# Expert down products moved behind the next block's gate and up products, with h kept in DRAM meanwhile

## The chip, the cores and the metric

The kernel runs on one core of a Trainium2 chip. The metric is the time of one launch in device microseconds: median 2381.64 us of three runs (2381.1 to 2393.33). All times below without a unit are microseconds.

## The reference

One layer of a decoder trunk for 1024 prompt rows and 8 decode rows, D = 1024: projection and two kinds of attention, a residual add, then a mixture of experts, a gated per-layer embedding and a last norm. The change touches what follows the attention:

```python
x = x + hier_moe(rmsnorm(x, g_moe), ...)        # 4 groups x 8 experts, top 2 inside the top group
gate = jax.nn.sigmoid(rmsnorm(x, g_ple) @ w_pg)
x = x + gate * (p @ w_pp);  y = rmsnorm(x, g_final)

def expert_block(args):                          # one block: 128 rows of one expert
    xi, ei = args
    return (jax.nn.silu(xi @ w_gate[ei]) * (xi @ w_up[ei])) @ w_down[ei]
```

`w_gate[e]` and `w_up[e]` are 1024 x 512 floats (2 MiB each), `w_down[e]` is 512 x 1024 (2 MiB). Every block brings its three matrices from HBM, whether or not its neighbour has the same expert.

## The kernel before

The program is a row of stages with a barrier of all engines between them. Four of them matter here: `residual` makes h (9 tiles of 128 rows, the last of 8) and the router's logits; `route` sorts the rows by expert and scatters them to `xs` in DRAM; `experts` works through the blocks; `finish` gathers each row's two results from `ys`, adds them to h and does the rest. h stays in SBUF from `residual` to `finish`.

In this profiled execution `experts` has 32 blocks, two to a turn of a hardware loop (the number comes from a register, `passes`). Each engine has its own in-order instruction stream, and semaphores join them. For block n:

- SP (the queue of loads, in order): x(n), two halves of w_gate, two of w_up, then w_down. The raw w_gate and w_up have one buffer each, so each half waits until VectorE has finished reading the last block's (`gl_full`, `ul_full`). w_down has two buffers and waits for the products of block n - 2.
- ScalarE makes the high parts (`high`: `wgh`, `wuh`, `xh`, type fp32r), VectorE the low parts (`low`: what is left after the high part is taken away). The gate and up products are three fp32r matmuls for each of 8 slices of the contraction (`products`, L86 to L88).
- TensorE (`step`, L1857): `gate_up(n-1)`, `turn(n)` (8 transposes of x), `down(n-1)`: 4 transposes of the hidden rows (L1847), then, when VectorE has copied them to `hT` (L1947), 8 plain fp32 matmuls into two banks (L1854; the profile records each as two).
- VectorE (`step`, L1949): `gated`, the first half of w_gate's low part, `hidden`, `hidden_T`, `turn`, the second half, `low_x`, then w_up's low parts.
- ScalarE copies the result to `y` (L1891), and GpSimd sends it to `ys` (L1981).

A matmul tile is named out<-moving,stationary: `x_Y<-x_wd,x_hT` streams the weights past the transposed hidden rows.

Of the kernel before, what the change touches and what calls it, by code (L numbers as in the profile page):

```python
# [19 lines left out]
P = 128  # L20
# [29 lines left out]
MAXBLK = (ASG + NE * (P - 1)) // P  # L50
NEG = -1.0e30
# [1381 lines left out]
def residual(nc, g, x_of):  # L1433

    ctx = ExitStack()
    with ctx:
# [3 lines left out]
        w = sb("r_w", [P, KD, D])  # L1440
        wr = sb("r_wr", [P, KD, NR])
# [14 lines left out]
        h, u2, logit, mT, ident = g["h"], g["u2"], g["logit"], g["mT"], g["ident"]  # L1456
# [4 lines left out]
        def _(sp):  # L1461
# [9 lines left out]
            for t in range(TT):  # L1471
                need(sp, h_full, t - 1)
                sp.dma_start(xt[0:rows(t), t % 2, :], x_of(t)).then_inc(x_in[t % 2], 16)

# [75 lines left out]
def route(nc, g):  # L1550
# [5 lines left out]
    with ctx:  # L1556
# [95 lines left out]
        def _(dve):  # L1652
# [85 lines left out]
            then(dve.tensor_scalar(metaf[:, 2:3], metaf[:, 2:3], -1.0, None, ALU.add))  # L1738
# [3 lines left out]
def experts(nc, g):  # L1742
# [6 lines left out]
    with ctx:  # L1749
# [17 lines left out]
        x_in, d_in = ([sem(f"{n}{b}") for b in range(2)] for n in ("x_in", "d_in"))  # L1767
        wg_in, wu_in = ([sem(f"{n}{b}") for b in range(2)] for n in ("wg_in", "wu_in"))
        gh_full, gl_full, uh_full, ul_full, xh_full, xl_full = map(sem, (
            "gh_full", "gl_full", "uh_full", "ul_full", "xh_full", "xl_full"))  # L1770
        HALVES = [slice(0, KD // 2), slice(KD // 2, KD)]
        y_out = g["pool_dma"][3:5]
        gm_in, tpx_full, xT_full, g_full, u_full, sg_full, gs_full, hm_full, tph_full, hT_full, y_full, y_read = map(
            sem, ("gm_in", "tpx_full", "xT_full", "g_full", "u_full", "sg_full", "gs_full", "hm_full", "tph_full",
                  "hT_full", "y_full", "y_read"))
        xs, ys, meta_row, ident = g["xs"], g["ys"], g["meta_row"], g["ident"]
        Wg = g["w_gate"].rearrange("a e (k p) f -> (a e) p k f", p=P)
        Wu = g["w_up"].rearrange("a e (k p) f -> (a e) p k f", p=P)
        Wd = g["w_down"].rearrange("a e (k p) f -> (a e) p k f", p=P)
        block = ctx.enter_context(nc.Block())  # L1780

        def pairs(eng):

            return eng.value_load(meta_row[0:1, 2:3], min_val=(-(-ASG // P) + 1) // 2 - 1,
                                  max_val=(MAXBLK + 1) // 2 - 1) + 1

        def passes(eng, step, end):


            n = pairs(eng)  # L1790
            for j in range(2):
                step(0, j)
            with eng.Fori(1, n) as it:
                for j in range(2):
                    step(it, j)
            if end:
                end(n)

        @block.sync
        def _(sp):  # L1800
            with nc.allow_non_contiguous_dma(reason="1024 gains, once"):
                sp.dma_start(gm[:, :], g["g_moe"].rearrange("a (k p) -> p (a k)", p=P)).then_inc(gm_in, 16)

            def step(it, b):
# [11 lines left out]
                need(sp, y_full, it * 4 + (2 * b - 2))  # L1816
# [5 lines left out]
        def _(pe):  # L1822
            def turn(it, b):

                pe.wait_ge(x_in[b], it * 16 + 16)
                for c in range(2):
                    need(pe, xT_full, it * 4 + (2 * b + c - 1))
                    for k in range(4):
                        last = pe.transpose(tpx[c][:, k, :], x[:, b, (c * 4 + k) * P:(c * 4 + k + 1) * P], ident[:, :])
                    last.then_inc(tpx_full, 1)  # L1830

            def gate_up(n):

                pe.wait_ge(xl_full, n + 1)
                need(pe, hm_full, n)
                for bank, wh, wl, cut, s in ((G, wgh, wgl, gl_full, g_full), (U_, wuh, wul, ul_full, u_full)):
                    pe.wait_ge(cut, n * 2 + 2)
                    for k in range(KD):
                        last = products(pe, bank[:, :], xh[:, k, :], xl[:, k, :], wh[:, k, :], wl[:, k, :],
                                        k == 0, k == KD - 1)  # L1840
                    last.then_inc(s, 1)

            def down(p_, b, n):
                pe.wait_ge(hm_full, n + 1)
                need(pe, hT_full, n)
                for k in range(KF):
                    last = pe.transpose(tph[:, k, :], hm[:, k * P:(k + 1) * P], ident[:, :])  # L1847
                last.then_inc(tph_full, 1)
                pe.wait_ge(d_in[b], p_ * 16 + 16)
                pe.wait_ge(hT_full, n + 1)  # L1850
                for c in range(2):
                    need(pe, y_read, n * 2 - 1 + c)
                    for k in range(KF):
                        last = pe.matmul(Y[c][:, :], hT[:, k, :], wd[:, b, k, c * 512:(c + 1) * 512],  # L1854
                                         start=(k == 0), stop=(k == KF - 1))
                    last.then_inc(y_full, 1)

            def step(it, j):
                behind = j or not isinstance(it, int)
                p_, b, n = (it, 0, it * 2) if j else (it - 1, 1, it * 2 - 1)  # L1860
                if behind:
                    gate_up(n)
                turn(it, j)
                if behind:
                    down(p_, b, n)

            def end(np_):
                gate_up(np_ * 2 - 1)
                down(np_ - 1, 1, np_ * 2 - 1)
# [4 lines left out]
        def _(act):  # L1874
# [12 lines left out]
            def output(p_, b, n):  # L1887
                act.wait_ge(y_out[b], p_ * 16 + 16)
                for c in range(2):
                    act.wait_ge(y_full, n * 2 + c + 1)  # L1890
                    act.activation(y[:, b, c * 512:(c + 1) * 512], Y[c][:, :], ACT.Copy).then_inc(y_read, 1)  # L1891

            def step(it, j):
                behind = j or not isinstance(it, int)
                p_, b, n = (it, 0, it * 2) if j else (it - 1, 1, it * 2 - 1)
                new = it * 2 + j
                if behind:
                    sigmoid(n)
                high(new, wg, wgh, wg_in, g_full, gh_full)
                act.wait_ge(xT_full, new * 2 + 2)  # L1900
                act.activation(xh[:, :, :], xT[:, :, :], ACT.Copy).then_inc(xh_full, 1)
                high(new, wu, wuh, wu_in, u_full, uh_full)
                if behind:
                    output(p_, b, n)

            def end(np_):
                sigmoid(np_ * 2 - 1)
                output(np_ - 1, 1, np_ * 2 - 1)
# [4 lines left out]
        def _(dve):  # L1913
            dve.wait_ge(gm_in, 16)

            def turn(n):
                need(dve, u_full, n)
                for c in range(2):
                    dve.wait_ge(tpx_full, n * 2 + c + 1)
# [8 lines left out]
            def low(n, half, w, wh, wl, high_full, full):  # L1928

                dve.wait_ge(high_full, n * 2 + half + 1)  # L1930
# [3 lines left out]
            def gated(n):  # L1934
                dve.wait_ge(sg_full, n + 1)
                dve.tensor_tensor(gs[:, :], sg[:, :], G[:, :], ALU.mult).then_inc(gs_full, 1)
# [7 lines left out]
            def hidden_T(n):  # L1944
                dve.wait_ge(tph_full, n + 1)
                need(dve, y_full, n * 2)
                dve.tensor_copy(hT[:, :, :], tph[:, :, :]).then_inc(hT_full, 1)  # L1947

            def step(it, j):  # L1949
                behind = j or not isinstance(it, int)  # L1950
                n, new = it * 2 - 1 + j, it * 2 + j
                if behind:
                    gated(n)
                low(new, 0, wg, wgh, wgl, gh_full, gl_full)
                if behind:
# [8 lines left out]
            def end(np_):  # L1964
                gated(np_ * 2 - 1)
                hidden(np_ * 2 - 1)
                hidden_T(np_ * 2 - 1)
# [4 lines left out]
        def _(pool):  # L1972
            def step(it, b):
                n = it * 2 + b
                row = pool.value_load(meta_row[0:1, bass.ds(n * 4 + 1, 1)], min_val=0, max_val=ASG)
                pool.wait_ge(y_read, n * 2 + 2)
                if b:
                    pool.wait_ge(y_out[0], it * 16 + 32)
                else:
                    pool.wait_ge(y_out[1], it * 16 + 16)  # L1980
                pool.dma_start(ys[bass.ds(row, P), :], y[:, b, :]).then_inc(y_out[b], 16)  # L1981

            def end(np_):
                for b in range(2):
                    pool.wait_ge(y_out[b], np_ * 16 + 16)
                pool.wait_ge(gm_in, 16)

            passes(pool, step, end)


def finish(nc, g, p_of, y_of):
# [3 lines left out]
    with ctx:  # L1995
# [4 lines left out]
        C = D // 2  # L2000
        wpgh, wpgl = (sb(n, [P, KD, D], F32R) for n in ("wpgh", "wpgl"))
# [27 lines left out]
        h, wt, dest, ys, ident = (g[n] for n in ("h", "wt", "dest", "ys", "ident"))  # L2029
# [12 lines left out]
        def _(sp):  # L2042
            with nc.allow_non_contiguous_dma(reason="1024 gains, once"):
                sp.dma_start(gp[:, :], g["g_ple"].rearrange("a (k p) -> p (a k)", p=P)).then_inc(gp_in, 16)
            for t in range(2):
                sp.dma_start(pt[0:rows(t), t % 2, :], p_of(t)).then_inc(p_in[t % 2], 16)
            for n, (raw, w, _, _) in enumerate(pieces):
                need(sp, wl_full, n - 2)
                sp.dma_start(raw, w).then_inc(piece_in[n], 16)
            sp.dma_start(gf[:, :], g["g_final"].unsqueeze(0).broadcast_to([P, D])).then_inc(gf_in, 16)  # L2050
# [114 lines left out]
        def _(dve):  # L2165
            dve.wait_ge(gp_in, 16)

            def mixed(t):

                r = rows(t)  # L2170
                dve.wait_ge(y_in[t % 2], 32 * (t // 2 + 1))
# [81 lines left out]
def build(nc, g):  # L2253
    ctx = ExitStack()
    with ctx:
# [11 lines left out]
        g["ys"] = nc.dram_tensor("ys", (SLOTS, D), F32, kind="Internal").ap()  # L2267
        g["meta"] = nc.dram_tensor("meta", (P, 4), I32, kind="Internal").ap()
# [22 lines left out]
        with nc.sbuf_tensor("u2", [P, TT, D], F32) as u2:  # L2291
# [18 lines left out]
            g["h"] = ctx.enter_context(nc.sbuf_tensor("h", [P, TT, D], F32, side="right"))  # L2310
# [40 lines left out]
```

## Time and profile before

| What | us |
|---|---|
| Median of the runs | 2381.64 |
| The profiled execution's own time | 2380.5 |
| Its span, first to last instruction | 2378.9 |
| First gate product of the expert stage starts | 1521.57 |
| Last copy of a down product starts | 2194.16 |

Busy shares of the span: TensorE 85%, its weight loads 66%, VectorE 46%, ScalarE 36%, GpSimd 12%. These are means over all stages. For the change the expert stage is read by itself: TensorE is busy about 95 of each 100 us there, and the 16 DMA engines have something to do for about 95% of it. A DMA engine counts as busy while it has a transfer open, so this share says more of how long transfers are open than of how much room is left; the GB/s beside it say what moved. Start times are microseconds from the span's start.

### The profile page before, as it was taken

Reading aid. Unit: us, or ns where it says so; the run is one execution under the profiler, and the core shown is the slowest. Engines: PE = TensorE matmul, PEld = TensorE weight load, DVE = VectorE, ACT = ScalarE, POOL = GpSimd, SP = SyncE. Lnnn points to the kernel's source line nnn. Section 1 sums busy time; section 2 is a strip of 40 time slices with the busy share of each in tenths; the row PEclk is TensorE's granted clock in tenths of the full one; section 3 lists DMA queues with packets and bytes.
Section 4 is the critical chain, followed back from the end, with each engine's and each line's share of the span. In section 5 each row is a group of like instructions: output and inputs, shape, how many; then the busy total and the mean of one; then the engine's idle time right before and its main releaser. Section 6 shows DMA issues by size and latency. Waiting matters only on the chain. (4 is left out here: it accounts for less than half of the span.)

```text
span 2378.9 us, 27707 instructions
## 1 busy us (share of the span) xinstructions
PE 2012.9 (85%) x10172; PEld 1572.0 (66%) x10172; DVE 1098.7 (46%) x1363; ACT 850.9 (36%) x1171; POOL 277.5 (12%) x356
## 2 busy tenths in 40 slices
PE   6999999698989879993288994499999999998598
PEld 5999999687878857772177452366666666665485
DVE  5212121255546545552342214466666666664564
ACT  4111111255546415450031100344444444452354
POOL 0110111143334310001012002100000000000210
PEclk8999999899999959896588996699999999999699
DMA  3343443434111042206334102999999999994530
GB/s 116 113 136 106 124 123 108 144 107 145 37 63 37 28 89 41 41 1 162 102 106 163 53 19 73 341 374 360 348 347 350 352 353 357 351 349 156 194 99 37
DMA packets 222238, 392.70 MB, mean 165 GB/s; under 512 B 29468, under 2 KB 100620, under 8 KB 222165
## 3 DMA queue, kind: packets, MB, share of 16 engines
q1 hardware_dynamic: 202916, 325.28, 40.3%
q0 software_dynamic: 14928, 50.60, 6.7%
q10 hardware_dynamic: 4320, 15.85, 1.7%
q8 instruction: 46, 0.75, 0.1%
q14 instruction: 28, 0.22, 0.0%
HBM read 321.02 MB, written 78.35 MB: 168 GB/s over the span
## 5 line engine op out<-in xcount | busy, mean ns | idle before, releaser
L1854 PE MATMUL x_Y<-x_wd,x_hT 128*128 128x512 f32 x512 | 229.8, 602 | 34.4 <-DVE x_hT L1947 34.4
L86 PE MATMUL p_acc<-uh,p_wl 128*128 128x344 f32 x720 | 234.9, 326 | 13.2 <-DVE ul L292 9.1
L88 PE MATMUL p_acc<-uh,p_wh 128*128 128x344 f32 x720 | 230.6, 320 | 0.0
L87 PE MATMUL p_acc<-ul,p_wh 128*128 128x344 f32 x720 | 230.4, 320 | 0.0
L1854 PEld LDWEIGHTS x_Y<-x_wd,x_hT 128*128 128x128 f32 x512 | 95.2, 191 | 150.1 <-issue 150.1
L304 DVE COPY p_zk<-p_tp 128x512 f32<-128x512 f32 (+1 forms) x90 | 44.2, 547 | 304.5 <-PE p_tp L225 304.5
L1932 DVE TENSOR_TENSOR x_wgl<-x_wg,x_wgh 128x2048 fp32r<-128x2048 f32 x64 | 146.3, 2286 | 69.9 <-ACT x_wgh L1885 69.9
L268 ACT ACTIVATE p_zc<-p_acc 128x344 f32<-128x344 f32 x90 | 41.2, 458 | 321.8 <-PE p_acc L88 321.8
L561 PE MATMUL g_acc<-uh,g_wl 128*128 128x344 f32 x384 | 131.2, 342 | 21.6 <-ACT u L594 19.5
L86 PEld LDWEIGHTS p_acc<-uh,p_wl 128*128 128x128 f32 x720 | 135.8, 189 | 18.1 <-issue 14.8
L1932 DVE TENSOR_TENSOR x_wul<-x_wu,x_wuh 128x2048 fp32r<-128x2048 f32 x64 | 143.5, 2282 | 0.0
L1485 PE MATMUL r_acc<-r_w,mT 128*128 128x512 f32 (+1 forms) x288 | 128.5, 606 | 10.0 <-DMA r_w<-in_w_out 10.0
L1885 ACT ACTIVATE x_wgh<-x_wg 128x2048 fp32r<-128x2048 f32 x64 | 118.9, 1906 | 49.1 <-DMA x_wg<-in_w_gate 49.1
L88 PEld LDWEIGHTS p_acc<-uh,p_wh 128*128 128x128 f32 x720 | 135.9, 189 | 0.0
L87 PEld LDWEIGHTS p_acc<-ul,p_wh 128*128 128x128 f32 x720 | 135.9, 189 | 0.0
L561 PE MATMUL g_acc<-ul,g_wh 128*128 128x344 f32 x384 | 129.7, 338 | 0.0
L561 PE MATMUL g_acc<-uh,g_wh 128*128 128x344 f32 x384 | 129.5, 337 | 0.0
L86 PE MATMUL x_G<-x_wgh,x_xl 128*128 128x512 f32 x256 | 114.8, 448 | 9.9 <-DVE x_xl L1926 9.9
L1885 ACT ACTIVATE x_wuh<-x_wu 128x2048 fp32r<-128x2048 f32 x64 | 118.4, 1896 | 0.1
L655 POOL TENSOR_TENSOR s_z<-s_z,s_w 128x1024 f32<-128x1024 f32 (+7 forms) x64 | 91.8, 1434 | 208.9 <-DVE s_w L682 208.9
L682 DVE TENSOR_TENSOR_SCAN s_w<-s_w,s_r 128x1024 f32<-128x1024 f32 (+7 forms) x64 | 86.8, 1356 | 54.9 <-ACT s_w L631 54.4
L820 PE MATMUL d_S<-d_k,d_q 64*128 64x256 f32 (+3 forms) x272 | 94.8, 499 | 17.4 <-DMA d_v<-ztok 16.9
(320 smaller groups left out, 4089.2 us busy)
## 6 DMA issues: line engine op xcount, KB each, us to landing
x_wg<-in_w_gate SPq DMA_DIRECT2D x64, 1024.0 KB, 7.3
x_wu<-in_w_up SPq DMA_DIRECT2D x64, 1024.0 KB, 7.3
x_wd<-in_w_down SPq DMA_DIRECT2D x32, 2048.0 KB, 12.1
x_x<-xs SPq DMA_DIRECT2D x32, 512.0 KB, 9.8
ys<-x_y POOLq DMA_DIRECT2D x32, 512.0 KB, 5.5
zT<-p_zc ACTq DMA_DIRECT2D x30, 516.0 KB, 3.4
p_w<-in_w_in SPq DMA_DIRECT2D x30, 512.0 KB, 5.5
ztok<-p_zk POOLq DMA_DIRECT2D x30, 512.0 KB, 4.6
```

The lines of the kernel that those rows point to most:

```text
L86: pe.matmul(out, w_low, m_high, start=first, stop=False)
L87: pe.matmul(out, w_high, m_low, start=False, stop=False)
L88: return pe.matmul(out, w_high, m_high, start=False, stop=last)
L304: dve.tensor_copy(zk[0:r, b, t0:t0 + m, :], tp[j % 2][0:r, 0:m, :]).then_inc(zk_full, 1)
L561: last = pe.matmul(acc[grp % 2][:, 0:NS], lhs[:, c % 2, kk, :], rhs[:, kk, t], start=(x == 0), stop=(x == M - 1), skip_group_check=True)
L655: pool.tensor_tensor(z[:, u % ZB, 0:n], z[:, u % ZB, 0:n], w[:, u % WB, 0:n], ALU.subtract).then_inc(al_full, 1)
L682: dve.tensor_tensor_scan(w[:, u % WB, 0:n][:, ::-1], w[:, u % WB, 0:n][:, ::-1], r[:, u % 2, 0:n][:, ::-1], 0.0, ALU.add, ALU.add).then_in ...
L820: last = pe.matmul(S[x // 2][:, c:c + n], q[:, b, x, i * P:(i + 1) * P], k[:, b, x, key:key + n], start=True, stop=True, skip_group_check= ...
L1485: last = pe.matmul(acc[t % 2][0:r, c * 512:(c + 1) * 512], mT[:, k, t * P:t * P + r], w[:, k, c * 512:(c + 1) * 512], start=(k == 0), stop ...
L1854: last = pe.matmul(Y[c][:, :], hT[:, k, :], wd[:, b, k, c * 512:(c + 1) * 512], start=(k == 0), stop=(k == KF - 1))
L1885: act.activation(wh[:, HALVES[half], :], w[:, HALVES[half], :], ACT.Copy).then_inc(full, 1)
L1932: dve.tensor_tensor(wl[:, s, :], w[:, s, :], wh[:, s, :], ALU.subtract).then_inc(full, 1)
```

## The change

1. TensorE works on three blocks at once. Its step n is `gate(n-1)`, `turn_hidden(n-2)`, `up(n-1)`, `turn(n)`, `down(n-2)`. Two steps (one block each) more are peeled from the loop (`PEEL = 2`), and the value that the loop length comes from is shifted (`MINPAIR`).
2. SP's w_down wait is on `d_used`, which `down` raises once per block; the number is still "all blocks up to n - 2".
3. VectorE does both halves of w_gate's low part before `hidden` and `turn`; `hidden_T` goes ahead of them.
4. ScalarE copies out block n - 3 first in its step n, and issues the DMA to `ys` itself, with the load of the row number from SBUF that this needs. GpSimd only waits at the end.
5. The contraction index is split "(p k)" instead of "(k p)" for all three weights, for the gains and for x and the hidden rows: a partition's rows of a half of w_gate lie side by side in DRAM (8 KiB instead of four runs of 2 KiB; w_down 16 KiB instead of four of 4 KiB), and the transposes read their stationary operand with a step of 8 (x) or 4 (hidden rows) floats instead of 1.
6. `residual` has its own h and stores each tile to `h_kept` in DRAM; `finish` loads it again, tiles 0 and 1 ahead of its weights, tiles 2 to 8 behind them and ahead of `gf` (the last norm's gains), and adds a wait for it in `mixed`.

```diff
 sync, experts
-                need(sp, y_full, it * 4 + (2 * b - 2))
+                need(sp, d_used, it * 2 + (b - 1))
                 sp.dma_start(wd[:, b, :, :], w(Wd)).then_inc(d_in[b], 16)
...
-        Wg = g["w_gate"].rearrange("a e (k p) f -> (a e) p k f", p=P)
+        Wg = g["w_gate"].rearrange("a e (p k) f -> (a e) p k f", p=P)
...
 tensor, experts
             def step(it, j):
-                behind = j or not isinstance(it, int)
-                p_, b, n = (it, 0, it * 2) if j else (it - 1, 1, it * 2 - 1)
-                if behind:
-                    gate_up(n)
-                turn(it, j)
-                if behind:
-                    down(p_, b, n)
+                one, two = lag(it, j, 1), lag(it, j, 2)
+                if one:
+                    gate(one[0])
+                if two:
+                    turn_hidden(two[0])
+                if one:
+                    up(one[0])
+                turn(it * 2 + j, j, it)
+                if two:
+                    down(*two)
...
 scalar, experts
+            def output(n, b, it):
+                act.wait_ge(d_used, n + 1)
...
+                row = act.value_load(meta_row[0:1, bass.ds(n * 4 + 1, 1)], min_val=0, max_val=ASG)
+                act.dma_start(ys[bass.ds(row, P), :], y[:, b, :]).then_inc(y_out[b], 16)
...
 vector, experts
-                low(new, 0, wg, wgh, wgl, gh_full, gl_full)
-                if behind:
-                    hidden(n)
-                    hidden_T(n)
-                turn(new)
-                low(new, 1, wg, wgh, wgl, gh_full, gl_full)
+                if two:
+                    hidden_T(two[0])
+                for half in range(2):
+                    low(new, half, wg, wgh, wgl, gh_full, gl_full)
+                if one:
+                    hidden(one[0])
+                turn(new)
                 low_x(new)
...
 sync, finish
             for n, (raw, w, _, _) in enumerate(pieces):
                 need(sp, wl_full, n - 2)
                 sp.dma_start(raw, w).then_inc(piece_in[n], 16)
+            for t in range(2, TT):
+                load_h(t)
             sp.dma_start(gf[:, :], g["g_final"].unsqueeze(0).broadcast_to([P, D])).then_inc(gf_in, 16)
```

On TensorE, in the loop of the kernel before, the end of the up products of a block and what follows (`x_tpx` is the transpose of the new block's x, `x_tph` of the hidden rows):

```order
2182 L88 MATMUL x_U<-x_wuh,x_xh 128x512
2183 L1825 ISA
2184 L59 ISA
2185 L1829 MATMUL x_tpx<-ident,x_x 128x128 x8
2186 L1847 MATMUL x_tph<-ident,x_hm 128x128 x4
2187 L1849 ISA
2188 L59 REGISTER_ALU
2189 L1854 MATMUL x_Y<-x_wd,x_hT 128x512 x8
```

The same engine in the changed kernel, the last peeled step:

```order
2203 L89 MATMUL x_G<-x_wgh,x_xh 128x512
2204 L1868 MATMUL x_tph<-ident,x_hm 128x128 x4
2205 L87 MATMUL x_U<-x_wuh,x_xl 128x512
...
2228 L89 MATMUL x_U<-x_wuh,x_xh 128x512
2229 L1843 MATMUL x_tpx<-ident,x_x 128x128 x8
2230 L1877 MATMUL x_Y<-x_wd,x_hT 128x512 x8
```

The transposes of the hidden rows and the down products that need them now have a block's up products between them, and the down products are those of one block earlier.

On VectorE, one block of the kernel before, from the gated product (`x_gs`) on:

```order
788 L1936 TENSOR_TENSOR x_gs<-x_sg,x_G 128x512
790 L1932 TENSOR_TENSOR x_wgl<-x_wg,x_wgh 128x2048
792 L1942 TENSOR_TENSOR x_hm<-x_gs,x_U 128x512
794 L1947 COPY x_hT<-x_tph 128x512
795 L1920 TENSOR_TENSOR x_xT<-x_tpx,x_gm 128x512
797 L1920 TENSOR_TENSOR x_xT<-x_tpx,x_gm 128x512
798 L1932 TENSOR_TENSOR x_wgl<-x_wg,x_wgh 128x2048
800 L1926 TENSOR_TENSOR x_xl<-x_xT,x_xh 128x1024
```

And in the changed kernel:

```order
800 L1974 TENSOR_TENSOR x_gs<-x_sg,x_G 128x512
802 L1985 COPY x_hT<-x_tph 128x512
804 L1969 TENSOR_TENSOR x_wgl<-x_wg,x_wgh 128x2048
806 L1969 TENSOR_TENSOR x_wgl<-x_wg,x_wgh 128x2048
807 L1980 TENSOR_TENSOR x_hm<-x_gs,x_U 128x512
808 L1957 TENSOR_TENSOR x_xT<-x_tpx,x_gm 128x512 x2
810 L1963 TENSOR_TENSOR x_xl<-x_xT,x_xh 128x1024
```

The second low part of w_gate has moved ahead of the hidden rows (`x_hm`) and of x's transposes (`x_xT`), which stand in front of `x_xl`, the last thing that a block's gate products wait for.

## Rows read from the trace of the kernel before

**Rows 1.** Windows: length, busy us (count) of PE, PEld, DVE, ACT, POOL, PEclk, DMA share, GB/s.
```profile
1522.00:1524.00 2.00, 2.00 (x6) 1.52 (x6) 2.00 (x2) 1.98 (x2) 0.00 (x0) 0.50 1.04 412
1700.00:1800.00 100.00, 94.74 (x364) 63.27 (x363) 65.25 (x49) 46.76 (x38) 2.66 (x5) 1.00 0.95 351
2186.00:2188.00 2.00, 2.00 (x4) 0.91 (x3) 0.00 (x0) 0.00 (x0) 0.00 (x0) 0.50 0.00 0
2250.00:2300.00 50.00, 50.00 (x241) 41.52 (x240) 34.17 (x45) 30.54 (x46) 9.54 (x7) 1.00 0.38 124
```

**Rows 2.** Waits of all engines, 1550 to 2160: who, releaser, total, times, longest.
```profile
PE x_Y L1854 <- DVE x_hT L1947: 31.5, 29, 1.4
```

**Rows 3.** Waits of SP, same stretch.
```profile
SPq L1815 <- DVE x_wgl L1932: 297.9, 58, 6.3
```

**Rows 4.** Timeline of one block: start, duration, engine, line, operation, tile, idle before.
```profile
1753.35 0.79 PE L86 MATMUL x_G<-x_wgh,x_xl 128*128 128x512 f32 x1
...
1764.94 1.03 PE L1829 MATMUL x_tpx<-ident,x_x 128*128 128x128 f32 x8
1765.97 0.66 PE L1847 MATMUL x_tph<-ident,x_hm 128*128 128x128 f32 x4
1767.48 1.28 DVE L1920 TENSOR_TENSOR x_xT<-x_tpx,x_gm 128x512 f32<-128x512 f32 x2
1767.80 7.13 PE L1854 MATMUL x_Y<-x_wd,x_hT 128*128 128x512 f32 x16 [1.18 <-DVE x_hT L1947]
1768.68 2.28 DVE L1932 TENSOR_TENSOR x_wgl<-x_wg,x_wgh 128x2048 fp32r<-128x2048 f32 x1
1768.79 1.06 ACT L1901 ACTIVATE x_xh<-x_xT 128x1024 fp32r<-128x1024 f32 x1 [4.97 <-DVE x_xT L1920]
1770.88 1.22 DVE L1926 TENSOR_TENSOR x_xl<-x_xT,x_xh 128x1024 fp32r<-128x1024 f32 x1
...
1774.37 0.79 PE L86 MATMUL x_G<-x_wgh,x_xl 128*128 128x512 f32 x1
```

**Rows 5.** SP's own timeline of the same stretch.
```profile
1755.97 0.46 SPq L1817 DMA_DIRECT2D x_wd<-in_w_down  x1
...
1764.51 6.98 SPq L1815 DMA_DIRECT2D x_wg<-in_w_gate  x2
```

**Rows 6.** Tile x_wg: its loads, from issue to landing.
```profile
DMA to landing us min/median/max: 4.9/7.3/14.1
```

**Rows 7.** Timeline, first block: ScalarE released by the two halves of w_gate.
```profile
1512.75 1.91 ACT L1885 ACTIVATE x_wgh<-x_wg 128x2048 fp32r<-128x2048 f32 x1 [46.79 <-DMA x_wg<-in_w_gate]
...
1515.42 1.91 ACT L1885 ACTIVATE x_wgh<-x_wg 128x2048 fp32r<-128x2048 f32 x1 [0.76 <-DMA x_wg<-in_w_gate]
```

**Rows 8.** Timeline: the first gate products, and the last block.
```profile
1521.57 0.79 PE L86 MATMUL x_G<-x_wgh,x_xl 128*128 128x512 f32 x1 [9.88 <-DVE x_xl L1926]
...
1526.85 0.46 PE L86 MATMUL x_G<-x_wgh,x_xl 128*128 128x512 f32 x1
...
2183.59 0.66 PE L1847 MATMUL x_tph<-ident,x_hm 128*128 128x128 f32 x4 [0.87 <-DVE x_hm L1942]
2185.30 8.83 PE L1854 MATMUL x_Y<-x_wd,x_hT 128*128 128x512 f32 x16 [1.06 <-DVE x_hT L1947]
...
2194.16 0.60 ACT L1891 ACTIVATE x_y<-x_Y 128x512 f32<-128x512 f32 x1 [2.84 <-PE x_Y L1854]
```

**Rows 9.** Page, DMA issues, one of the last stage: KB each, us to landing.
```profile
f_gf<-in_g_final SPq DMA_DIRECT2D x1, 512.0 KB, 9.0
```

**Rows 10.** Timelines of SP, VectorE and TensorE in the last stage.
```profile
2230.84 0.47 SPq L2050 DMA_DIRECT2D f_gf<-in_g_final  x1
...
2242.70 1.22 DVE L2194 TENSOR_TENSOR f_uT<-f_tp,f_gp 128x1024 f32<-128x1024 f32 x1
...
2250.70 0.75 DVE L2186 TENSOR_SCALAR f_un<-h,f_st 128x1024 f32<-128x1024 f32 x1
...
2251.53 1.07 PE L2084 MATMUL f_tp<-ident,f_un 128*128 128x128 f32 x8
```

More of the change, by code:

```diff
@@ L50 @@
 MAXBLK = (ASG + NE * (P - 1)) // P
+MINPAIR = (-(-ASG // P) + 1) // 2
 NEG = -1.0e30
@@ L1780, in experts @@
         block = ctx.enter_context(nc.Block())
-        def pairs(eng):
-            return eng.value_load(meta_row[0:1, 2:3], min_val=(-(-ASG // P) + 1) // 2 - 1,
-                                  max_val=(MAXBLK + 1) // 2 - 1) + 1
+        PEEL = 2
         def passes(eng, step, end):
[L1790 to L1793, printed above, removed]
+            n = eng.value_load(meta_row[0:1, 2:3], min_val=0, max_val=(MAXBLK + 1) // 2 - MINPAIR) + MINPAIR
+            for it in range(PEEL):
+                for j in range(2):
+                    step(it, j)
+            with eng.Fori(PEEL, n) as it:
@@ L1797, in passes, with lag @@
                 end(n)
+        def lag(it, j, back):
+            new = it * 2 + j
+            if isinstance(it, int) and new < back:
+                return None
+            return new - back, (j - back) % 2, it + (j - back) // 2
         @block.sync
@@ L1830, in turn, with gate_or_up, gate @@
                     last.then_inc(tpx_full, 1)
-            def gate_up(n):
+            def gate_or_up(n, bank, wh, wl, cut, full):
+                for k in range(KD):
+                    if k % 4 == 0:
+                        pe.wait_ge(cut, n * 2 + (k // 4 + 1))
+                    last = products(pe, bank[:, :], xh[:, k, :], xl[:, k, :], wh[:, k, :], wl[:, k, :],
+                                    k == 0, k == KD - 1)
+                last.then_inc(full, 1)
+            def gate(n):
                 pe.wait_ge(xl_full, n + 1)
+                need(pe, gs_full, n)
+                gate_or_up(n, G, wgh, wgl, gl_full, g_full)
@@ L1835, in gate_up, with up @@
+            def up(n):
                 need(pe, hm_full, n)
[L1836 to L1843, printed above, removed]
+                gate_or_up(n, U_, wuh, wul, ul_full, u_full)
@@ L1871, in _ @@
+                if two:
[5 more added lines that the diff above has]
+                    down(*two)
+            def end(np_):
+                last = np_ * 2 - 1
+                gate(last)
+                turn_hidden(last - 1)
+                up(last)
+                down(last - 1, 0, np_ - 1)
+                turn_hidden(last)
+                down(last, 1, np_ - 1)
             passes(pe, step, end)
@@ L1964, in end @@
             def end(np_):
-                gated(np_ * 2 - 1)
-                hidden(np_ * 2 - 1)
-                hidden_T(np_ * 2 - 1)
+                last = np_ * 2 - 1
+                gated(last)
+                hidden_T(last - 1)
+                hidden(last)
+                hidden_T(last)
             passes(dve, step, end)
@@ L1972, in _ @@
         def _(pool):
[L1973 to L1988, printed above, removed]
+            np_ = pool.value_load(meta_row[0:1, 2:3], min_val=0, max_val=(MAXBLK + 1) // 2 - MINPAIR) + MINPAIR
+            for b in range(2):
+                pool.wait_ge(y_out[b], np_ * 16)
+            pool.wait_ge(gm_in, 16)
 def finish(nc, g, p_of, y_of):
@@ L2000, in finish @@
         C = D // 2
+        h = sb("h", [P, TT, D])
+        hs_in = [sem(f"h_in{t}") for t in range(TT)]
         wpgh, wpgl = (sb(n, [P, KD, D], F32R) for n in ("wpgh", "wpgl"))
```

102 lines of the change are left out of this document (59 added, 43 removed).

## The prediction

> **What bounds the kernel now.** I read the windows first, to find the stage that the change works in: in the middle of the expert stage TensorE is busy 94.7 of 100 us at full clock, while 351 GB/s move [rows 1]. The waits come next: TensorE's one wait there is for the copy of the transposed hidden rows, 29 times, 31.5 us together [rows 2]; it never waits for a weight. The timeline of one block gives its step [rows 4]: gate and up products 1753.35 to 1764.94 (11.59), transposes of x 1.03, transposes of the hidden rows 0.66, the wait up to 1767.80 (1.17), down products to the next gate product at 1774.37 (6.57). Together 21.02, of which 19.85 are work. So the stage is bound by TensorE, and the reader should see in [rows 3] why loads never matter: SP waits only for VectorE to free the raw weights, never for the down products. The w_down of a block goes out at 1755.97 and the next block's w_gate at 1764.51 [rows 5].
>
> The expert stage lasts from 1521.57 to the end of the last copy at 2194.76, 673.2 us [rows 8].
>
> **What the new order of TensorE gives.** The hidden rows' transposes are followed by up products of 5.8 us instead of by products that need their copy. The 1.17 wait is hidden. If that were all, a step would last 19.85, and 31 blocks would give back about 36 us. Total work is the same: the down products are the same 8 plain fp32 matmuls.
>
> **What it takes: SP.** Call D the end of the down products of block n - 2. In the kernel before they end in TensorE's step n - 1; now they end in step n, one step later, while SP's wait for them still stands at the same place, in front of w_down(n). Behind this wait in SP's order are x(n+1) and both halves of w_gate(n+1), whose buffers VectorE freed long before. They used to leave then; now they leave at D, and behind 2.10 MB of w_down and 0.52 MB of x. ScalarE's result DMA (0.52 MB) is issued after its two copies, at about D + 3, and shares the engines in just this stretch. From D to the first gate product of block n + 1:
>
> - issue and latency 2.2: the quickest w_gate half took 4.9 [rows 6], of which 1.05 MB at 393 GB/s (the two halves of the first block landed 2.67 apart, [rows 7]) are 2.7;
> - 2.10 + 0.52 + 2.10 + 0.52 = 5.24 MB. The rate for rows of 8 and 16 KiB isn't in the trace. With rows of 2 and 4 KiB it was 393 by the landings and 412 in the best window [rows 1, 7]; at 393 it would be 13.3; larger rows may gain as much again over 412 as that is above 393 (431), which gives 12.2. I take 405, between the two measured ones: 12.9;
> - high part of the second half 1.91 [rows 7], its low part 2.28, then on VectorE the hidden rows 0.65 (the size of one of x's two, 1.28 for both), x's transposes 1.28, on ScalarE xh 1.06, on VectorE xl 1.22 [rows 4]; hand-overs of some 0.1 each, 0.4. Together 8.8.
>
> Sum 23.9. TensorE would be ready for that gate product at D + 19.85, so it waits 4.1. It comes in every second interval: D(n-2) holds back gate n+1, whose step ends with D(n) 19.85 later. Two blocks last 19.85 + 23.9 = 43.8 at least, against 42.0 now.
>
> **The clock.** In the last block TensorE stood 0.87 and 1.06 around 0.66 of work, and then ran the next stretch at a granted clock of 0.50, the 1.2 GHz level [rows 1, 8]; its 16 down records took 8.83 instead of 7.13, 1.7 lost. At the stage's start 12 gate products at this level took 5.28 (1521.57 to 1526.85) instead of 2.80, 2.5 lost. The gaps of 1.2 in the middle of the stage leave the clock at 1.00 [rows 1]. A wait of 4.1 is longer than the last block's two together, so I expect the fall each time, and 2.0 lost, between the two rows. Bounds: 0 and 2.5.
>
> **The sum of the stage.** Behind w_gate(0), in at 1515.4 [rows 7], come w_up(0), w_down(0), x(1) and w_gate(1), 6.8 MB, so w_gate(1) is in at 1515.4 + 6.8 / 0.405 = 1532.2, and with 8.8 the second gate product starts at 1541.0. The third starts at 1560.9. From there to the 32nd: 15 intervals of 23.9 + 2.0 and 14 of 19.85 give 666.4, so 2227.3. Then 11.59 + 0.66 + 6.57 + 0.66 + 1.17 + 7.13, and 1.2 for two copies after the end: 29.0, ending at 2256.3. That is 61.5 later than 2194.76.
>
> **Transposes with a step of 8 and 4 floats.** Each is 0.13 (1.03 / 8) now [rows 4]; no row has a strided stationary operand. Bounds: nothing, and twice the time, 1.69 more in a step. It would count only in the interval that TensorE bounds: 15 times, 25 us. I take nothing, as in the nearest rows. The Trainium skill (SBUF — State Buffer, Specifications (TRN2), Cachelines) says that a 16-byte line has to be hit at least twice for full bandwidth and that each cross to a new line pays a penalty; both steps cross at every float. By this rule the strided transposes would be slower, which is the last rival below; no row here bears it out or refutes it.
>
> **Result rows from ScalarE.** Two copies, a register load and an issue fit ahead of the sigmoid: ScalarE is busy 46.8 of 100 us [rows 1]. I take nothing beyond the 0.52 MB counted above; if they came late they would hold up the sigmoid, which has until D + 15 before it matters. GpSimd's queue held nothing else.
>
> **h through DRAM.** The stores (4.2 MB) lie in `residual`, beside TensorE's work: nothing; the last lands some 3 us after h is made, and the stage still works on logits then. In the last stage tiles 0 and 1 arrive beside the gathers: nothing, at most 2.6 (1.05 MB). But tiles 2 to 8 (3.18 MB) now go out in front of `gf`, which was issued at 2230.84 and took 9.0, so it landed at 2239.8 [rows 9, 10]. VectorE waits for it in front of the loop. It began at 2242.70; with 3.18 MB at 0.405, 7.9 later, gf lands at 2247.7, and VectorE starts 5.0 late. Its un of tile 2 (ended 2251.45) met TensorE's transposes at 2251.53 with 0.08 to spare, and TensorE is busy all of the next 50 us [rows 1, 10]. So 5.0 are added, and 0 to 2.5 for the clock: 6.5.
>
> **Sum.** 2380.5 (the profiled execution's time; its span is 2378.9, and the median is 1.1 above it) + 61.5 + 6.5 = 2448.5; I say 2448.
>
> **Rivals.**
>
> - The clock stays at its upper level over the waits of 4 us. For it: the wait is a single one, and between waits TensorE is busy without a break. Against it: the last block. Then 15 x 2.0 and 1.5 less: 2417.
> - SP's wait binds nothing and TensorE bounds the stage. Faster. Place: the gate product after D. It holds if the second half of w_gate(n+1) lands by D + 11.0 (19.85 - 8.8), where I count 15.1. For it: two blocks' worth of time look like enough slack, large rows may move faster than any row here, and 351 GB/s are less than 412. Against: even at 431 GB/s and without the result rows it is D + 2.2 + 11.0. Then 1560.9 + 29 x 19.85 + 29.0 = 2165.6, 29.2 earlier, with 6.5 lost at the end: 2358.
> - Between: the loads land at about D + 13, without the result rows in their way; a wait of 2 us that leaves the clock alone. 15 x 21.8: 1560.9 + 327 + 277.9 + 29.0 = 2194.8, as before, with the 6.5 of the last stage: 2387.
> - Slower still: transposes at twice the time on top of the forecast, 2448 + 25 = 2473.
>
> The Trainium skill (DMA: Bandwidth & Descriptors, Where 436 GB/s comes from) puts the ceiling of the DMA ports at 435 GB/s. With that instead of 405 the long interval would be 0.9 shorter and the forecast 13 less; the windows here reach 412.
>
> **How the numbers follow.** Forecast 0.50, full clock 0.20, the faster case 0.12, the one between 0.08, slow transposes 0.10. A measurement of this kernel can tell about 0.5%, 12 us. The faster case alone is faster (0.12); the one between falls on both sides of 2394, mostly in no change (0.06); the rest is slower (0.82). The range reaches from 2386, which leaves out the faster case and a little of the one between, to 2474. The likeliest case's own range is 2425 to 2465.
>
> **What would show it.** SP waiting for TensorE's x_Y in front of x_wd, 29 times some 14 to 16 us; x_wg's two issues close together right behind x_x. TensorE waiting for VectorE's x_xl in front of x_G, about 15 times 4 us, long and short block intervals alternating (near 26 and 20); granted clock under 1.00 in windows of the stage. No wait for x_hT within the loop. In the last stage VectorE held at f_uT until 2247 + the shift of the stage. x_tpx in 1.03 or not. The prediction is wrong if SP doesn't wait for TensorE, or if w_gate lands within 11 us of D.

## The result and the profile after

| | median, us | runs |
|---|---|---|
| before | 2385.80 | 2381.10 to 2393.33, 4 |
| after | 2472.81 | 2463.96 to 2478.21, 4 |

The ratio is 1.0358, 95% interval 1.0313 to 1.0403: slower. The forecast of 2448 had the direction and lies 25 under the median. The median is inside the stated range of 2386 to 2474, by 1.2, and above the likeliest case's own range of 2425 to 2465, by 8. The profiled execution of after took 2478.21, its span is 2476.6. Two more executions of each kernel were profiled later, to see what of the difference repeats. Cut at the same four places (the first load of x, the first gate product, the end of the last copy of a down product, the first load of the last stage), the spans read:

| Piece | before, 3 executions | after, 3 executions | mean difference | forecast |
|---|---|---|---|---|
| up to the first load of x | 1506.1, 1525.2, 1521.2 | 1529.7, 1530.8, 1513.2 | +7.1 | 0 |
| first load to first gate product | 15.5, 15.5, 16.0 | 16.6, 17.1, 16.9 | +1.2 | 0 |
| first gate product to the end of the last copy | 673.2, 672.9, 673.1 | 740.9, 736.3, 735.7 | +64.6 | +61.5 |
| end of the last copy to the last stage's first load | 6.8, 6.8, 6.8 | 3.9, 3.9, 3.9 | -2.9 | 0 |
| last stage | 177.3, 177.3, 177.7 | 185.5, 186.8, 185.1 | +8.4 | +6.5 |

The pieces from the first load of x on repeat, within 0.5 in before and 5.2 in after. They add up to +71.3, against 68.0 in the forecast. The piece ahead of them does not repeat, and takes up the rest.

The middle of the expert stage, windows of after (columns as in [rows 1]):

```profile
1700.00:1800.00 100.00, 86.96 (x315) 60.23 (x316) 59.31 (x45) 45.69 (x37) 0.00 (x0) 0.92 0.82 325
...
1748.00:1750.00 2.00, 0.23 (x1) 0.23 (x2) 1.23 (x1) 2.00 (x3) 0.00 (x0) 1.00 1.02 434
1750.00:1752.00 2.00, 2.00 (x6) 1.57 (x6) 1.88 (x1) 2.00 (x3) 0.00 (x0) 0.57 0.89 379
1752.00:1754.00 2.00, 2.00 (x7) 1.53 (x6) 2.00 (x2) 0.85 (x2) 0.00 (x0) 0.58 1.06 440
```

TensorE is busy 87 of 100 us where it was 95, at 0.92 of full clock where it had 1.00, and the DMA engines moved 325 GB/s where they moved 351. Nothing is nearer its limit than before; everything waits more. The waits of after, from 1560 to 2230 (who waits <- for whom, total, times, longest):

```profile
ACT x_wgh L1916 <- DMA x_wg<-in_w_gate: 105.2, 29, 7.2
PE x_G L87 <- DVE x_xl L1963: 72.3, 15, 5.1
```

And those of SP's queue in the same stretch, which answer to [rows 3]:

```profile
SPq L1830 <- PE x_Y L1877: 440.2, 28, 17.1
SPq L1828 <- DVE x_wul L1969: 85.9, 30, 6.5
```

The wait of [rows 2] for `x_hT` is gone. In its place TensorE waits every second block for `x_xl`, and behind that ScalarE waits for the w_gate load itself. The load is late because SP stood in front of w_down for up to 17.1. One block of SP, then of ScalarE and VectorE, then of TensorE, each in order of time (start, duration, engine, line, operation, tile, idle before); they answer to [rows 4, 5]:

```profile
1725.67 0.33 SPq L1830 DMA_DIRECT2D x_wd<-in_w_down  x1
1727.51 0.33 SPq L1824 DMA_DIRECT2D x_x<-xs  x1
1728.10 0.91 SPq L1828 DMA_DIRECT2D x_wg<-in_w_gate  x2
...
1745.09 0.33 SPq L1830 DMA_DIRECT2D x_wd<-in_w_down  x1
```

```profile
1738.68 1.91 ACT L1916 ACTIVATE x_wgh<-x_wg 128x2048 fp32r<-128x2048 f32 x1 [6.81 <-DMA x_wg<-in_w_gate]
1741.16 1.92 ACT L1916 ACTIVATE x_wgh<-x_wg 128x2048 fp32r<-128x2048 f32 x1 [0.57 <-DMA x_wg<-in_w_gate]
...
1743.11 2.29 DVE L1969 TENSOR_TENSOR x_wgl<-x_wg,x_wgh 128x2048 fp32r<-128x2048 f32 x1 [0.19 <-ACT x_wgh L1916]
1745.32 0.68 DVE L1980 TENSOR_TENSOR x_hm<-x_gs,x_U 128x512 f32<-128x512 f32 x1
1745.91 1.28 DVE L1957 TENSOR_TENSOR x_xT<-x_tpx,x_gm 128x512 f32<-128x512 f32 x2
...
1748.32 1.23 DVE L1963 TENSOR_TENSOR x_xl<-x_xT,x_xh 128x1024 fp32r<-128x1024 f32 x1 [1.12 <-ACT x_xh L1937]
```

```profile
1749.77 0.50 PE L87 MATMUL x_G<-x_wgh,x_xl 128*128 128x512 f32 x1 [4.71 <-DVE x_xl L1963]
...
1763.08 1.05 PE L1843 MATMUL x_tpx<-ident,x_x 128*128 128x128 f32 x8
1763.96 7.03 PE L1877 MATMUL x_Y<-x_wd,x_hT 128*128 128x512 f32 x16
...
1770.43 0.80 PE L87 MATMUL x_G<-x_wgh,x_xl 128*128 128x512 f32 x1
```

Read it from the top: w_down leaves as soon as the products two blocks back are done (1725.67); the second half of w_gate is in at 1741.16, 15.5 later; then 8.6 of conversions up to the gate product at 1749.77, which is 24.1 after SP was let go. The next gate product, at 1770.43, waits for nothing.

### The profile page after: what moved, and what is told of

Same layout as the page of the kernel before. It is cut to its first block and busy times, and to the rows that moved or that the text cites. A ratio compares the mean times of both kernels' runs of the same rounds, so it can differ in the third digit from the quotient of the medians.

```text
span 2476.6 us, 27666 instructions
## 1 busy us (share of the span) xinstructions
PE 2063.3 (83%) x10172; PEld 1617.0 (65%) x10172; DVE 1101.1 (44%) x1363; ACT 852.8 (34%) x1172; POOL 260.7 (11%) x323
## 5 line engine op out<-in xcount | busy, mean ns | idle before, releaser
L87 PE MATMUL x_G<-x_wgh,x_xl 128*128 128x512 f32 x256 | 125.0, 488 | 88.1 <-DVE x_xl L1963 88.1
L87 PEld LDWEIGHTS x_G<-x_wgh,x_xl 128*128 128x128 f32 x256 | 57.3, 224 | 117.9 <-issue 88.3
L821 PE MATMUL d_S<-d_k,d_q 64*128 64x256 f32 (+3 forms) x272 | 105.5, 544 | 17.6 <-DMA d_v<-ztok 17.1
L88 PE MATMUL x_G<-x_wgl,x_xh 128*128 128x512 f32 x256 | 115.6, 452 | 0.0
```

Of the source, the lines that this page charges most:

```text
L87: pe.matmul(out, w_low, m_high, start=first, stop=False)
L88: pe.matmul(out, w_high, m_low, start=False, stop=False)
L821: last = pe.matmul(S[x // 2][:, c:c + n], q[:, b, x, i * P:(i + 1) * P], k[:, b, x, key:key + n], start=True, stop=True, skip_group_check= ...
```

## The experiments

A variant is told by its edit to the changed kernel unless it says otherwise. Differences of whole runs are against the before that ran on the same chip.

**1. SP's wait moved to where it holds nothing back.** SP issues w_down of the last block behind this block's w_up; the same loads, one place apart.

```diff
 sync, experts, step n
-                need(sp, d_used, it * 2 + (b - 1))
-                sp.dma_start(wd[:, b, :, :], w(Wd)).then_inc(d_in[b], 16)
+                if not (isinstance(it, int) and it == 0 and b == 0):
+                    down_weights(n - 1, 1 - b)
+            def down_weights(n, b):
+                e = sp.value_load(meta_row[0:1, bass.ds(n * 4, 1)], ...)
+                need(sp, d_used, n - 1)
+                sp.dma_start(wd[:, b, :, :], Wd[bass.ds(e, 1), :, :, :]...).then_inc(d_in[b], 16)
```

> The changed kernel, with one load moved in SP's order: w_down(n-1) is issued behind x, w_gate and w_up of block n, instead of w_down(n) there; its wait is still for the down products of the block two before it, which have then ended a step earlier. Theory A (SP stands in front of w_down until the down products end, and holds w_gate back behind it): SP's wait for x_Y goes, TensorE's wait for x_xl in front of x_G goes, all block intervals are near 19.85, the granted clock stays 1.00; the expert stage takes about 644 from its first gate product to its last copy instead of some 740; the whole kernel 95 to 105 less than the changed one where the stages ahead of the experts take the same. Rival B (the stage is bound by what the DMA engines move, or by the chain over ScalarE and VectorE): the interval stays at 21.5 or more, and the kernel gains less than half of this. The time ahead of the expert stage was 24 longer in the changed kernel's profile, in stages that it leaves alone. If that comes with the program (theory P), it is there again here, 1504 or so for the store of the block table instead of 1480; if it is chance (theory C), it lies anywhere from 1480 to 1504.

Measured: 2357.97 (2355.51 to 2359.71), ratio to before 0.9842, interval 0.9778 to 0.9906. The stage from first gate product to last copy took 632.1 instead of after's 735.7 to 740.9. Waits of SP and the window, 1700 to 1800:

```profile
SPq L1828 <- DVE x_wul L1975: 237.2, 58, 6.5
SPq L1828 <- DVE x_wgl L1975: 148.6, 58, 5.0
SPq L1835 <- PE x_Y L1883: 13.7, 1, 13.7
```

```profile
1700.00:1800.00 100.00, 100.00 (x394) 69.49 (x393) 68.80 (x53) 52.59 (x42) 0.00 (x0) 1.00 0.95 381
```

One wait for TensorE is left of 28. TensorE is busy all of the time at full clock, all intervals between gate products from the third on are 19.4 (the expectation had 19.85, and 644 for the stage), and the same loads now move at 381 GB/s. So the wait in SP's queue was the whole of the loss in the stage, and the new order (of TensorE, VectorE and ScalarE, which changed together) is worth 41 there (673.1 to 632.1) once it is lifted.

**2. The same, with gf's load ahead of the loads of h.**

```diff
 sync, finish
+            sp.dma_start(gf[:, :], ...).then_inc(gf_in, 16)
             for t in range(2, TT):
                 load_h(t)
-            sp.dma_start(gf[:, :], ...).then_inc(gf_in, 16)
```

> As the run with the late w_down, and in the last stage gf is loaded ahead of tiles 2 to 8 of h. Theory A (VectorE waits for gf, which stands behind 3.18 MB of h): its wait of some 6 for gf goes, TensorE's wait of 6 for un goes, and the last stage (from the load of f_gp to the end) takes 177, as in the kernel before, instead of 185: 8 less than the run with the late w_down. Rival: then h(2) or the second rows of p are late instead, and the gain is under 4.

Measured: 2352.27 (2340.77 to 2367.42), ratio 0.9826 (0.9746 to 0.9906). The last stage took 176.9 instead of 185.8 in experiment 1. That is all that the loads of h cost there: 8.9. In the whole run the 5.7 is less than the two intervals can tell.

**3. The same as experiment 1, with h left in SBUF.** `h_kept` and its stores and loads are taken out; residual and finish share h again, as in the kernel before.

```diff
 residual, finish
-                sp.dma_start(g["h_kept"][...], h[...]).then_inc(h_out, 16)
...
-            for t in range(2, TT):
-                load_h(t)
```

> As the run with the late w_down, with h kept in SBUF all the time as in the kernel before: no stores, no loads. By theory A the last stage takes 177 (8 less than with the late w_down alone), everything else as there; the whole kernel about 30 to 35 less than the kernel before by its stages (644 against 673), so 2350 to 2360 by a median, if the stages ahead take the same. If keeping h in DRAM bought something in the expert stage, this run's expert stage is longer than that of the run with the late w_down.

Measured: 2343.59 (2340.49 to 2367.09), ratio 0.9779 (0.9716 to 0.9842); last stage 177.4, expert stage 632.6. Another execution, on another chip, took 2352.03, where before ran at a median of 2397.97. It beats both kernels. Its median is the lowest of all, but the interval overlaps that of experiment 2, and in the two stages the two are alike (631.7 and 176.9 there). The order of TensorE didn't need h's room.

**4. Experiment 1 with the short rows and unit steps of before.** Every "(p k)" back to "(k p)".

```diff
-        Wg = g["w_gate"].rearrange("a e (p k) f -> (a e) p k f", p=P)
+        Wg = g["w_gate"].rearrange("a e (k p) f -> (a e) p k f", p=P)
```

> As the run with the late w_down, with the contraction index split as before: 2 and 4 KiB rows, transposes with unit steps. Theory A: with SP's wait away TensorE bounds the stage, loads of 7.34 MB in 19.85 are 370 GB/s, under the 393 to 412 that these rows reached, so the interval is 19.9 to 20.3 and the stage within 6 of the run with the late w_down. Rival: the long rows are what makes the loads fit; then the interval is 20.5 or more and w_gate lands late. Weight loads of the transposes go back from 0.19 to 0.14, and nothing comes of it.

Measured: 2356.08 (2350.00 to 2369.11), ratio 0.9855 (0.9783 to 0.9927); stage 631.1 against 632.1: no difference where TensorE bounds the stage, and 19.4 between gate products in both. What the strided transposes do is seen in the records of tile `x_tpx` (ns min/median/max), in experiment 1, with a step of 8 floats, and here, with a step of 1:

```profile
L1849 PEld LDWEIGHTS x_tpx<-ident,x_x x256: 185/192/226, 1522.4 to 2132.6; 128*128 128x128 f32 x128
L1849 PE MATMUL x_tpx<-ident,x_x x256: 270/274/475, 1522.4 to 2132.7; 128*128 128x128 f32 x128
```

```profile
L1849 PEld LDWEIGHTS x_tpx<-ident,x_x x256: 138/141/230, 1512.0 to 2122.0; 128*128 128x128 f32 x128
L1849 PE MATMUL x_tpx<-ident,x_x x256: 271/273/473, 1512.0 to 2122.2; 128*128 128x128 f32 x128
```

The weight load takes 0.192 instead of 0.141, still beside a matmul record of 0.27, which doesn't change.

**5. The kernel before, with its w_down wait one block later.** The order of TensorE and everything else is that of before; only the wait is for the products of block n - 1 instead of n - 2.

```diff
 sync, experts (the kernel before)
-                need(sp, y_full, it * 4 + (2 * b - 2))
+                need(sp, y_full, it * 4 + 2 * b)
```

> The kernel before, with nothing changed but SP's wait in front of w_down(n): it waits for the down products of block n - 1, which end in TensorE's step n as those of block n - 2 do in the changed kernel. Theory A: the late wait alone costs, whatever order TensorE has. SP waits about 29 times for x_Y, w_gate(n+1) lands 12 to 15 after the end of the down products, block intervals alternate between about 21.0 and 24.5 to 26, the stage gets 50 to 80 longer, and the kernel is slower by 2 to 3.4%. Rival B (the new order of TensorE or VectorE is what loses the time): within 10 of the kernel before.

Measured: 2679.69 (2674.19 to 2689.46), ratio 1.1205 (1.1171 to 1.1240). The sign was expected, the size was missed by a factor of about four. Its waits, 1600 to 2150, and then one step of its timeline, rows of SP, ScalarE, VectorE and TensorE:

```profile
ACT x_wgh L1885 <- DMA x_wg<-in_w_gate: 153.1, 36, 8.0
PE x_tph L1847 <- DVE x_hm L1942: 115.1, 18, 6.4
```

```profile
1900.55 0.99 SPq L1815 DMA_DIRECT2D x_wg<-in_w_gate  x2
...
1911.86 1.91 ACT L1885 ACTIVATE x_wgh<-x_wg 128x2048 fp32r<-128x2048 f32 x1 [7.63 <-DMA x_wg<-in_w_gate]
1913.81 2.29 DVE L1932 TENSOR_TENSOR x_wgl<-x_wg,x_wgh 128x2048 fp32r<-128x2048 f32 x1 [8.85 <-ACT x_wgh L1885]
...
1916.01 0.68 DVE L1942 TENSOR_TENSOR x_hm<-x_gs,x_U 128x512 f32<-128x512 f32 x1
1916.75 0.71 PEld L1847 LDWEIGHTS x_tph<-ident,x_hm 128*128 128x128 f32 x4 [6.62 <-DVE x_hm L1942]
...
1918.84 9.78 PE L1854 MATMUL x_Y<-x_wd,x_hT 128*128 128x512 f32 x16 [0.97 <-DVE x_hT L1947]
...
1928.65 0.37 SPq L1817 DMA_DIRECT2D x_wd<-in_w_down  x1
```

In before's order VectorE does the first low part of w_gate(n+1) ahead of `x_hm` of block n [the order of VectorE is in the section on the change]. The down products of block n need that `x_hm`, and SP's next w_down, with w_gate(n+2) behind it, needs those products. So the loop closes within one step, in every block: 30.7 between gate products each time, never a short one, and the stage took 966.2. The expectation had carried over the changed kernel's loop, which closes over two steps. The down products also ran at the lower clock level behind the wait (9.78 instead of 7.13).

**6. ScalarE sends the result rows later.** Its register load and DMA go behind the high parts of w_gate instead of right behind the copies.

```diff
 scalar, experts
             def output(n, b, it):
...
+            def send(n, b, it):
                 row = act.value_load(meta_row[0:1, bass.ds(n * 4 + 1, 1)], ...)
                 act.dma_start(ys[bass.ds(row, P), :], y[:, b, :]).then_inc(y_out[b], 16)
...
                 high(new, wg, wgh, ...)
+                if three:
+                    send(*three)
```

> The changed kernel, with ScalarE's DMA of the result rows issued behind the high parts of w_gate instead of ahead of the sigmoid. Theory A with its byte term (0.52 MB of result rows share the DMA engines between the end of the down products and the landing of w_gate): the long way from w_down's issue to the gate product two later, 24.1 in the changed kernel, gets 1.2 shorter, and so do 15 pairs: 15 to 20 less in all. Rival: the result rows don't hold the loads up, and nothing changes (within 5).

Measured: 2412.48 (2404.64 to 2421.71), ratio 1.0097 (1.0063 to 1.0132), stage 692.2: 44 to 49 less than after, two to three times what was expected. TensorE's wait, 1560 to 2190:

```profile
PE x_G L87 <- DVE x_xl L1970: 40.5, 15, 3.1
```

The way from SP's release to the gate product is 22.3 instead of 24.1: the 0.52 MB (1.3 at 405) and half a us more. The waits are 2.7 instead of 4.8 each, 32 less together. The rest, some 14, is clock: only 8 of the 14 intervals that follow a wait are 20.7, and the others 19.2 to 19.5 (one of 20.4 has a wait of 0.8 in it), where after has 20.7 or 21.8 each time. The expectation had the transfer right within half a us and the clock left out.

**7. The changed kernel with short rows.** The edit of experiment 4, on after, where the loads bound every second interval.

> The changed kernel, with the contraction index split as before: rows of 2 and 4 KiB for the weights, unit steps in the transposes, and SP's late wait in place. Theory A with its byte term: 5.24 MB stand between the end of the down products and the gate product two later, at 395 to 412 instead of the 434 to 440 that the changed kernel's best windows show, so this way is 0.7 to 1.2 longer than 24.1, and the stage 10 to 20 longer. Rival: the length of the rows makes no difference to the rate (within 3 in the stage), as it made none where the wait in front of w_down was moved away (631.1 against 632.1).

Measured: 2477.20 (2472.47 to 2480.95), ratio 1.0328 (1.0278 to 1.0378). Stage 753.1, that is 12 to 17 longer than after's three, as expected (10 to 20). SP's release and ScalarE's start on the second half:

```profile
1716.73 0.37 SPq L1830 DMA_DIRECT2D x_wd<-in_w_down  x1
```

```profile
1733.27 1.91 ACT L1916 ACTIVATE x_wgh<-x_wg 128x2048 fp32r<-128x2048 f32 x1 [0.80 <-DMA x_wg<-in_w_gate]
```

16.5 instead of 15.5, with SP's issues at the same distances behind the release, within 0.1: the long rows save 1.0 in each interval that waits for loads, and nothing where none does (experiment 4).

**8 to 12. Both kernels again.** No edit; two more profiled executions of each, and one of experiment 3.

> The kernel before, a second look. Theory C (the 24 ahead of the experts are chance, the granted clock in the dilated attention): the block table's store lies somewhere else than at 1480, by 5 to 20, with the dilated stage longer or shorter at a lower or higher granted clock. Theory P: 1480 within 3.

> The changed kernel, a second look. Theory P: the block table's store at 1504 within 3. Theory C: somewhere else by 5 to 20. The expert stage and the last stage as in the first profile, within 3.

> A third look at the changed kernel. Theory C (the dilated stage's length is a matter of the execution): one of the lengths seen so far in any kernel, 288, 294, 299 or 309, and not 309 a third time with any certainty. Theory P (it belongs to the program): 309.

> A third look at the kernel before, which had 288.0 and 299.6 in the dilated stage. Theory C: one of 288, 294, 299 or 309. The expert stage 673 and the last stage 177.3 within 1.

> A second look at the kernel with the late w_down and h in SBUF, which had 308.7 in the dilated stage. Theory C: it may be any of the lengths seen; theory P: 309 again. The expert stage 632 and the last stage 177 within 1.

Measured: before 2399.29 and 2396.41, after 2476.50 and 2456.43, experiment 3 2352.03. The stage whose code is the same in all of them, one of the two kinds of attention, in windows that hold all of it, for before, before again, after and after for the third time:

```profile
856.00:1144.00 288.00, 228.91 (x1296) 176.01 (x1296) 136.35 (x218) 101.05 (x191) 10.41 (x32) 0.83 0.29 64
```

```profile
864.00:1164.00 300.00, 240.82 (x1298) 184.36 (x1299) 137.10 (x219) 101.12 (x191) 10.46 (x32) 0.79 0.27 60
```

```profile
860.00:1169.00 309.00, 251.48 (x1296) 192.41 (x1296) 136.39 (x218) 101.24 (x191) 10.42 (x32) 0.76 0.26 60
```

```profile
858.00:1151.00 293.00, 234.51 (x1296) 179.83 (x1296) 136.52 (x218) 101.15 (x191) 10.46 (x32) 0.81 0.28 62
```

The work is the same: 1296 matmuls, 136 us of VectorE, 101 us of ScalarE. Only TensorE's busy time and its granted clock differ, 228.9 at 0.83 to 251.5 at 0.76. Before took 288 and 300, after 309, 309 and 293, experiment 3 309 and 300. So most of the profiled pair's 23.6 ahead of the experts is not due to the change. The other experiments settle the rest. Up to the first load of x, experiments 1, 2, 4, 6 and 7 run the changed kernel's code. With them its eight executions lie between 1508.3 and 1530.8, mean 1518.7; the kernel before and experiment 5 lie between 1506.1 and 1525.2, mean 1518.5; experiment 3, with before's `residual`, has 1535.2 and 1520.1. So the 7.1 of the table is spread as well, and the stores of h cost nothing that can be seen there. The expert stage of after's second execution was expected within 3 of the first one's, and was 4.6 shorter.

## Why the prediction was right, and where 25 us went

**The new order of TensorE.** Right: the wait for the hidden rows is hidden. The step is 19.4, not 19.85, since the durations of neighbouring records overlap: the 8 transposes are put down with 1.05, but the down products start 0.88 after them (1763.08 to 1763.96), and the down products hold TensorE 6.47, not 6.57. Start to start is the better reading. Without SP's wait the order gave 41 back (experiment 1), where the prediction put about 36.

**SP's queue.** Right, and the heart of it. Forecast from release to gate product 23.9, measured 23.9 to 24.5: the second half in at D + 15.5 where 15.1 was said, the conversions 8.6 where 8.8 was said. Experiment 1 shows the cause by taking it away, and experiment 6 shows the result rows' share in it. Not forecast: D, as SP sees it, comes 0.6 behind the start of the next gate product (1771.03 against 1770.43). That and the shorter step cancel nearly: from the fourth gate product to the 32nd, two blocks took 46.1, 45.8 and 45.7 in the three executions, against 45.75.

**The rate.** 405 GB/s was a fair mean: 5.24 MB in 15.5 less 2.2 is 394. The windows above have 434 and 440, where before's had 412; but the way is set by all of the 13 us, from the first bytes to the last, and not by the best two. Windows of 2 us don't give the rate well either: each transfer is counted whole in the window in which it starts, and others of this trace read up to 459. Over 10 us the best windows of the changed kernel and of experiment 7 (long and short rows) are:

```profile
1553.00:1563.00 10.00, 8.35 (x40) 6.71 (x39) 6.37 (x6) 4.20 (x3) 0.00 (x0) 1.00 1.03 434
```

```profile
1581.00:1591.00 10.00, 10.00 (x41) 6.77 (x40) 1.49 (x3) 1.95 (x2) 0.00 (x0) 1.00 1.04 403
```

The Trainium skill (DMA: Bandwidth & Descriptors, Where 436 GB/s comes from) has a ceiling of 435 GB/s for the ports; the trace agrees, with 434 as the most over 10 us. The kernel before has 409, experiment 4 has 412.

**The clock.** Right: 0.57 behind each wait of some 4.8. The cost falls into the following interval, 20.7 or 21.8 instead of 19.4, so 1.3 or 2.4, mean 1.8, against 2.0 (the repeats have some of 20.4 too, and means of 1.7 and 1.6). One such cost was forgotten: the second block's gate product came behind a wait of 4.7 as well. The one behind the 32nd gate product is among the 15 that the sum has, but the sum books it ahead of that product; it shows in the end, 31.1 (2256.1 to 2287.2) where the sum has 29.0.

**The stage.** 61.5 forecast, 64.6 in the mean of three. From the first gate product to the third it took 40.4 where the sum has 39.3, from there to the 32nd 669.5, 666.1 and 664.4 (mean 666.7) where it has 666.4, and from there to the end 31.1, 29.8 and 30.8 where it has 29.0. The first gate product itself, 1.2 later behind the first load of x, isn't accounted for by any experiment.

**The strided transposes.** Nothing, as taken. The Trainium skill (SBUF — State Buffer, Specifications (TRN2), Cachelines) predicted a penalty, and there is one, 0.05 for each weight load; it costs nothing, since the load lies beside the matmul. The rival at 2473, though near the median, is refuted by experiment 4.

**The last stage.** The step that was too small: 6.5 forecast, 8.4 measured. SP, VectorE and TensorE in after's last stage, one row each, answering to [rows 10]:

```profile
2324.37 0.35 SPq L2087 DMA_DIRECT2D f_gf<-in_g_final  x1
```

```profile
2338.99 1.22 DVE L2232 TENSOR_TENSOR f_uT<-f_tp,f_gp 128x1024 f32<-128x1024 f32 x1 [6.29 <-DMA f_gf<-in_g_final]
```

```profile
2347.80 1.97 PE L2121 MATMUL f_tp<-ident,f_un 128*128 128x128 f32 x8 [5.95 <-DVE f_un L2224]
```

Counted from the stage's first load (2201.6 in before, 2291.1 in after), gf was there at 38.2 in before [rows 9, 10] and at 47.9 here: 9.7 later, where the sum has 7.9. So the 3.18 MB cost as much as they would at 328 GB/s, and not at the 405 carried over from the expert stage. Of the 9.7, 0.4 is that the last weights landed later; tile 2 landed 2.5 behind them, and tiles 3 to 7 1.3 to 1.6 apart (0.52 MB each). VectorE starts at 47.9 instead of 41.1, and TensorE's transposes of tile 2 at 56.7 instead of 49.9, 6.8 late where 5.0 was forecast. The other 1.6 of the 8.4 go with the clock (the eight transposes took 1.97 instead of 1.07), for which 1.5 had been taken. Experiments 2 and 3 both take it all back, 8.9 and 8.4. Not forecast, and the other way: the last stage begins 2.9 sooner after the last copy. ScalarE sends the rows there instead of GpSimd, but no experiment takes this by itself.

**What was left.** From the first load of x on the forecast was 3.3 too low. Most of the other 21 of the 25 us lies ahead of it: the sum was built on an execution of before, 2380.5, with one of the shortest attention stages seen (288) and its first load of x at 1506.1, and two of after's three have the longest (309), with a mean of 1524.6 for that load. That is 18.5; the last 3 are the distance from these executions to the median. The likeliest case was right in its mechanism, and the spread between executions belonged in its range. That the median is still inside the stated range is in part luck: the range reached up to 2474 for the sake of slow transposes, which did not come, and not for this spread.

## What to carry to other kernels

When a consumer is moved one step later, look for every wait on it and at what stands behind that wait in its queue: here one wait on SP, for the same block as before, held back two other loads and turned a gain of 41 us into a loss of 65. Move the load together with the products that free its buffer; here the wait then cost nothing, with nothing else changed. Before a loop bound is carried over to another order, follow it once around through every engine: whether it closed over two steps or one made 65 or 293 us in the stage.

## What the runs showed of the hardware

- Identical work took 228.9 to 251.5 us of TensorE in one stage, at a mean granted clock of 0.83 to 0.76, from one execution to another, and up to 21 us of the total with it.
- Behind a wait of 4.5 to 5.1 TensorE was granted the lower level (1.2 GHz) each time, with a cost of 1.0 to 2.5; behind one of 2.8 to 3.1 in 7 of 14 cases (experiment 6).
- A transpose whose stationary operand has a step of 8 floats loads in 0.192 instead of 0.141; with 4 floats in 0.203 instead of 0.140. The matmul records are 0.274 instead of 0.273 and 0.283 instead of 0.272, and a step of TensorE stayed at 19.4.
- Loads with rows of 8 and 16 KiB for the weights reached 434 GB/s over 10 us, those with 2 and 4 KiB rows 403 to 412, and the long ones delivered the same 5.24 MB 1.0 sooner.
